# Unread matmuls in TensorE's pauses, the reciprocal roots spread from their column, and sums moved to VectorE, in a two-layer hybrid decoder trunk on one core

## The reference

```
for l in range(2):
    sh1, sc1, g1, sh2, sc2, g2 = split(silu(c) @ w_mod[l] + b_mod[l])
    p = (x * (1 + sc1) + sh1) @ w_in[l]                 # q k v qi ki wi xr yg
    attn = dsa_attention(rope(q), rope(k), v, ...)      # 4 heads, top 128 keys per query
    lru  = rg_lru(conv(xr)) * gelu(yg)                  # 512 wide
    merged = concat(rms_norm(attn, g_attn), rms_norm(lru, g_lru))
    x = layer_norm(alpha * x + (1 + g1) * (merged @ w_out[l]))
    h2 = x * (1 + sc2) + sh2
    x = layer_norm(alpha * x + (1 + g2) * (square(relu(h2 @ w_up[l])) @ w_down[l]))
```

## Time and profile before

| | |
|---|---|
| median of 3 runs | 1364.4 us (1359.66 to 1368.24) |
| the profiled execution | 1368.02 us, of which 1366.2 us are the span from its first to its last instruction |
| TensorE busy | 1300.0 us, 95% of the span |
| VectorE, ScalarE, GpSimd busy | 789.9, 552.0, 156.6 us |
| mean granted TensorE clock | 0.966 of full |
| HBM read | 155.64 MB, 115 GB/s over the span |

### The profile page before, as it was taken

How to read it: one execution, slowest core, us unless ns; L and a number is a source line. 1 busy time by engine, 2 the same in 40 slices (tenths; PEclk the granted TensorE clock), 3 DMA queues, 4 the chain that set the end, 5 groups by cost and what they waited for, 6 DMA issues and landing times.

```text
span 1366.2 us, 17071 instructions
## 1 busy us (share of the span) xinstructions
PE 1300.0 (95%) x6225; PEld 1025.0 (75%) x6225; DVE 789.9 (58%) x1298; ACT 552.0 (40%) x849; POOL 156.6 (11%) x129
## 2 busy tenths in 40 slices
PE   3999998899999999999999999988999999999996
PEld 2776766776888888888867776657868888888886
DVE  3656988556752734537466589874574344343353
ACT  3743455533632413324246335563273232231331
POOL 3000334001000000000120013510200000000012
PEclk9999998898999999999989999989999999999997
DMA  9743445211334243342244444520223323333311
GB/s 314 250 157 124 154 128 187 71 47 47 109 121 140 92 154 96 104 154 93 77 140 153 141 126 136 171 76 10 84 62 123 93 92 99 101 92 93 104 64 62
DMA packets 73397, 158.56 MB, mean 116 GB/s; under 512 B 6528, under 2 KB 10872, under 8 KB 73336
## 3 DMA queue, kind: packets, MB, share of 16 engines
q1 hardware_dynamic: 59904, 108.61, 25.5%
q0 software_dynamic: 12800, 48.76, 10.7%
q10 hardware_dynamic: 632, 0.39, 0.1%
HBM read 155.64 MB, written 2.10 MB: 115 GB/s over the span
## 4 chain that ended last, share of the span: by engine, by line
PE 90%; ACT 3%; DVE 3%; DMA 2%; issue 1%; POOL 0%; POOLq 0%; DVEq 0%; SPq 0%; ACTq 0%
PE bank L645 26%; PE bank L647 25%; PE bank L646 25%; PE bank L690 2%; DMA first_mod<-in_w_mod_dram 2%; PE bank L610 2%; PE bank L548 1%; PE bank L834 1%; PE bank L868 1%; PE bank L742 1%; PE bank L848 1%; DVE lru_gate L1694 1%; PE bank L878 1%; PE bank L905 1%; PE bank L568 1%
## 5 line engine op out<-in xcount | busy, mean ns | idle before, releaser
L1440 DVE TENSOR_TENSOR w_lo<-w_raw,w_hi 128x1024 fp32r<-128x1024 f32 (+1 forms) x192 | 207.7, 1098 | 340.5 <-ACT w_hi L984 340.5
L984 ACT ACTIVATE w_hi<-w_raw 128x1024 fp32r<-128x1024 f32 (+1 forms) x216 | 203.7, 960 | 469.7 <-PE bank L647 467.7
L645 PE MATMUL bank<-a_hi,w_hi 128*128 128x512 f32 x896 | 374.4, 418 | 9.6 <-DVE a_lo L1482 6.3
L646 PE MATMUL bank<-a_lo,w_hi 128*128 128x512 f32 x896 | 352.4, 393 | 0.0
L647 PE MATMUL bank<-a_hi,w_lo 128*128 128x512 f32 x896 | 352.2, 393 | 0.0
L645 PEld LDWEIGHTS bank<-a_hi,w_hi 128*128 128x128 f32 x896 | 170.0, 190 | 64.0 <-issue 26.7
L646 PEld LDWEIGHTS bank<-a_lo,w_hi 128*128 128x128 f32 x896 | 170.3, 190 | 40.9 <-issue 5.8
L645 PE MATMUL bank<-b_hi,w_hi 128*128 128x512 f32 x512 | 199.7, 390 | 0.0
L647 PE MATMUL bank<-b_hi,w_lo 128*128 128x512 f32 x512 | 199.3, 389 | 0.0
L646 PE MATMUL bank<-b_lo,w_hi 128*128 128x512 f32 x512 | 199.2, 389 | 0.0
L647 PEld LDWEIGHTS bank<-a_hi,w_lo 128*128 128x128 f32 x896 | 170.0, 190 | 36.9
(11 more groups left out here) (265 smaller groups left out, 1473.7 us busy)
## 6 DMA issues: line engine op xcount, KB each, us to landing
mod_raw<-in_w_mod_dram POOLq DMA_DIRECT2D x40, 1024.0 KB, 5.9
w_raw<-in_w_up_dram SPq DMA_DIRECT2D x64, 512.0 KB, 3.7
w_raw<-in_w_down_dram SPq DMA_DIRECT2D x64, 512.0 KB, 3.7
w_raw<-in_w_in_dram SPq DMA_DIRECT2D x48, 512.0 KB, 3.7
w_raw<-in_w_out_dram SPq DMA_DIRECT2D x16, 512.0 KB, 3.8
first_mod<-in_w_mod_dram SPq DMA_DIRECT2D x4, 1024.0 KB, 19.6
first_mod<-in_w_mod_dram POOLq DMA_DIRECT2D x4, 1024.0 KB, 15.2
x_in<-in_x_dram POOLq DMA_DIRECT2D x4, 512.0 KB, 14.4
```

The source lines that it names most:

```text
L645: mm(o, wh, hi(kk), start=first, stop=False)
L646: mm(o, wh, lo(kk), start=False, stop=False)
L984: last = af(hi, src, ACT.Copy)
L1440: last = tt(lo, src, hi.bitcast(F32), ALU.subtract)
```

## The change

Six edits, of which the first two are one idea.

1. `keep_busy(n, b)` issues n matmuls of 512 columns of an fp32r identity into a bank that nobody reads. `layer_norm` has 3 of them after the sums of `ln_q`, and 14 (`LN_FILL`) after the spread of the roots. Each of the units 0 to 7 of the attention has 2 ahead of `turned(u)`.
2. `spread` no longer multiplies `ones_d` by a diagonal. Four matmuls of 128 columns have one column of roots as their weights, read with a stride of 0, and the identity as the moving operand. `diag` and `diag_l` go; the semaphore `roots_ready` takes the place of `diag_done`.
3. VectorE adds the eighth tile too into `ln_s` (not for the last norm). TensorE has four one-column matmuls less in the sums and one 128x512 matmul less for the mean. The sums now come in the order `ln_q`, `ln_s`, last squares.
4. VectorE adds the four tiles of squares of the recurrent branch into one at units 12, 13 and 14; `lru_sums` has 4 matmuls instead of 16 and stands at unit 15.
5. The modulation pieces 14 and 15 stand after the attention units and after the spread for the recurrent branch instead of at units 6 and 9.
6. In `norms` the low part of tile 0 comes before `norm_tile(1)`.

```
+LN_FILL = 14
 def spread(b, name, l, src):
-    mm(banks[b][:, :], ones_d[:, :], src.rearrange("p t q -> p (t q)"), start=True, stop=True)\
-        .then_inc(full_s[b], 1)
+    for t in range(TT):
+        last = mm(banks[b][:, t * P:(t + 1) * P], src[:, t:t + 1].broadcast_to([P, P]), ident[:, :], start=True, stop=True)
+    last.then_inc(full_s[b], 1)
+
+def keep_busy(n, b=6):
+    for _ in range(n):
+        mm(banks[b][:, :], ident_r[:, :], ident_r[:, :].unsqueeze(1).broadcast_to([P, TT, P]), start=True, stop=True)
...
 def layer_norm(l, tail, n):
-    x_last = x[:, DK - 1, :]
+    pe.wait_ge(ln_q_s, n * (DK - 2) + 2)
+    pe.wait_ge(free_s[4], uses_before(4, "sums" + tail, l))
+    add(TT, ln_q, first=True)
+    pe.wait_ge(free_s[6], ...)          # bank 6 of the group before is read
+    keep_busy(3)
     pe.wait_ge(ln_s_s, n)
-    pe.wait_ge(free_s[4], uses_before(4, "sums" + tail, l))
-    add(0, ln_s, first=True)
-    pe.wait_ge(ln_q_s, n * (DK - 2) + 2)
-    add(TT, ln_q)
-    pe.wait_ge(free_s[7], ...)
-    add(0, x_last)
+    add(0, ln_s)
     pe.wait_ge(ln_sq_s, n * DK)
     add(TT, ln_sq[:, (DK - 1) % 2, :], stop=True).then_inc(full_s[4], 1)
     pe.wait_ge(free_s[5], uses_before(5, "mb" + tail, l))
-    mm(banks[5][:, :], ones_d[:, :], ln_s[:, :], start=True, stop=False)
-    mm(banks[5][:, :], ones_d[:, :], x_last, start=False, stop=True).then_inc(full_s[5], 1)
-    pe.wait_ge(diag_done, l * 3 + (3 if tail else 2))
-    spread(4, "rb" + tail, l, diag)
+    mm(banks[5][:, :], ones_d[:, :], ln_s[:, :], start=True, stop=True).then_inc(full_s[5], 1)
+    pe.wait_ge(roots_ready, l * 3 + (3 if tail else 2))
+    spread(4, "rb" + tail, l, stat[:, 3, :])
+    keep_busy(LN_FILL)
...
-    pe.wait_ge(sq_ready, l * LT + LT)
+    pe.wait_ge(sq_added, l * (LT - 1) + (LT - 1))
     for t in range(TT):
-        for m in range(LT):
-            last = mm(banks[4][:, t:t + 1], sq_l[:, m, ...], ones_d[:, 0:1], start=(m == 0), stop=(m == LT - 1))
+        last = mm(banks[4][:, t:t + 1], sq_l[:, 0, ...], ones_d[:, 0:1], start=True, stop=True)
...
-        if u in (3, 6, 9):
-            late_mod(l, 12 + u // 3)
-        if u == 14:
+        if u == 3:
+            late_mod(l, 13)
+        if u == 15:
             lru_sums()
+        if u < 8:
+            keep_busy(2, 4)
         turned(u)
...
+    late_mod(l, 14)
     turn_tile(0)()
     turn_tile(1)()
-    pe.wait_ge(diag_done, l * 3 + 1)
-    spread(4, "lrb", l, diag_l)
+    pe.wait_ge(roots_ready, l * 3 + 1)
+    spread(4, "lrb", l, mix_root[:, 0:TT])
+    late_mod(l, 15)
     group("out0", ...)
...
 # VectorE: ln_stats, the attention units, norms
-    step(v_.reciprocal(stat[:, 3, :], stat[:, 2, :]))
-    step.settle()
-    stt(diag[:, :, :], ident..., float(D), stat[:, 3, :]..., ALU.mult, ALU.mult).then_inc(diag_done, 1)
+    v_.reciprocal(stat[:, 3, :], stat[:, 2, :]).then_inc(roots_ready, 1)
...
+    if 12 <= u < 12 + LT - 1:
+        m = u - 11
+        ve.wait_ge(sq_ready, l * LT + (m + 1))
+        ...
+        tt(sq_l[:, 0, :], sq_l[:, 0, :], sq_l[:, m, :], ALU.add).then_inc(sq_added, 1)
...
     norm_tile(0)
     first_full(l, blk)
-    norm_tile(1)
     step.settle()
     a_lo_tile(l, blk, 0)
+    norm_tile(1)
```

More of the change, by code:

```diff
@@ L226, in trunk_kernel @@
         full = sb("unsplit", [P, 2, T], F32, full_at)
-        diag = sb("diag", [P, TT, P], F32, full_at)
-        diag_l = sb("diag_lru", [P, TT, P], F32, yg_at)
         mod_rows = sb("mod_rows", [P, T], F32, yg_at + K2)
@@ L294, in trunk_kernel @@
         attn_max, mask_ready = sem("attn_max"), sem("mask_ready")
-        attn_sq, root_diag_s = sem("attn_squared"), sem("root_diag_done")
+        attn_sq, root_diag_s = sem("attn_squared"), sem("root_roots_ready")
         lru_squared = sem("decay_squared")
         pv_done = sem("pv_done")
-        sq_ready = sem("squares_ready")
+        sq_ready, sq_added = sem("squares_ready"), sem("squares_added")
         ln_sq_s, ln_q_s, ln_s_s = sem("ln_squared"), sem("ln_q_added"), sem("ln_s_added")
         var_done, root_done = sem("var_done"), sem("root_done")
-        diag_done = sem("diag_done")
+        roots_ready = sem("roots_ready")
         loads_begun, turns_begun = sem("loads_begun"), sem("turns_begun")
@@ L744, in add @@
                     return last
-                x_last = x[:, DK - 1, :]
-                pe.wait_ge(ln_s_s, n)
-                pe.wait_ge(free_s[4], uses_before(4, "sums" + tail, l))
-                add(0, ln_s, first=True)
-                pe.wait_ge(ln_q_s, n * (DK - 2) + 2)
-                add(TT, ln_q)
[L752 to L755, removed]
-                add(0, x_last)
+                pe.wait_ge(ln_q_s, n * (DK - 2) + 2)
+                pe.wait_ge(free_s[4], uses_before(4, "sums" + tail, l))
+                add(TT, ln_q, first=True)
+                pe.wait_ge(free_s[6], uses_before(6, "down12", l, NC - 1) + 1 if tail else uses_before(6, "out12", l) + 1)
+                keep_busy(3)
+                pe.wait_ge(ln_s_s, n)
+                add(0, ln_s)
                 pe.wait_ge(ln_sq_s, n * DK)
@@ L872, in lru_sums @@
                 def lru_sums():
-                    pe.wait_ge(sq_ready, l * LT + LT)
+                    pe.wait_ge(sq_added, l * (LT - 1) + (LT - 1))
                     pe.wait_ge(free_s[4], uses_before(4, "lms", l))
                     for t in range(TT):
-                        for m in range(LT):
-                            last = mm(banks[4][:, t:t + 1], sq_l[:, m, t * P:(t + 1) * P], ones_d[:, 0:1],
-                                      start=(m == 0), stop=(m == LT - 1))
+                        last = mm(banks[4][:, t:t + 1], sq_l[:, 0, t * P:(t + 1) * P], ones_d[:, 0:1], start=True, stop=True)
                     last.then_inc(full_s[4], 1)
@@ L883, in layer @@
                 pe.wait_ge(rope_done, l * 13 + 13)
-                pe.wait_ge(free_s[4], uses_before(4, f"vt{HEADS - 1}", l) + 1)
+                pe.wait_ge(free_s[4], uses_before(4, "lms", l))
                 scores(0)
@@ L1531, in ln_sum @@
                     ins = tt(ln_s[:, :], ln_s[:, :], x[:, m, :], ALU.add)
-                    if m == DK - 2:
+                    if m == (DK - 2 if name == "down1" and l == DEPTH - 1 else DK - 1):
                         ins.then_inc(ln_s_s, 1)
@@ L1739, in layer @@
                         lru_scan(u - 7)
+                    if 12 <= u < 12 + LT - 1:
+                        m = u - 11
+                        ve.wait_ge(sq_ready, l * LT + (m + 1))
+                        if m > 1:
+                            ve.wait_ge(sq_added, l * (LT - 1) + (m - 1))
+                        tt(sq_l[:, 0, :], sq_l[:, 0, :], sq_l[:, m, :], ALU.add).then_inc(sq_added, 1)
                     if u in (6, 10, 14):
@@ L1795, in layer @@
                 token_diag(1)
-                stt(diag_l[:, :, :], ident[:, :].unsqueeze(1).broadcast_to([P, TT, P]), float(D),
-                   mix_root[:, 0:TT].unsqueeze(2).broadcast_to([P, TT, P]), ALU.mult, ALU.mult).then_inc(diag_done, 1)
+                ve.sem_inc(roots_ready, 1)
                 mix_vars(2)
@@ L1838, in run @@
                             residual(l, f"out{j}", m, 2)
-                            if m < DK - 1:
-                                ln_sum(l, f"out{j}", m)
+                            ln_sum(l, f"out{j}", m)
                     return run
@@ L1875, in run @@
                                 residual(l, f"down{j}", m, 5, c)
-                                if last and m < DK - 1:
+                                if last and (m < DK - 1 or l < DEPTH - 1):
                                     ln_sum(l, f"down{j}", m, c)
```

2 lines of the change are left out of this document (removed).

## The result

The changed kernel takes 1348.18 us (median of 4 runs, 1347.46 to 1349.79) against 1366.32 us (4 runs, 1359.66 to 1368.41): a ratio of 0.9876, 95% interval 0.9848 to 0.9904, so 18 us or 1.2% faster. The profiled execution took 1348.19 us with a span of 1346.3, 19.9 us less than the profiled execution of before, whose 1368.02 us were at the upper end of its runs. So a comparison of the two traces shows some 2 us more than the medians do.

The account below looks back on a forecast made before the run. The prediction took TensorE, 90% of the chain, as the bound, through its standstills and half-clock stretches. Norms 12.0, attention's end 9.1 and start 0 sum to 21.1 us; between 1346.9 and 1343.3 it took 1345 us, range 1338 to 1354.

Parts of the forecast that it names:

- Group starts after the norms: At the three norms, the next matmul group starts at E + 9.2, E ending the last group's matmuls; 6.7 us saved.
- Clock behind the norms: In the groups after the three norms, full clock instead of half gives back 6.4 us.
- the sum of 14.7: Whole-kernel saving instead of 21.1 us if recorded clock events were unreliable and the 6.4 us behind the norms dropped out.
- Can the group use it? ... yes, barely: Groups after norms: TensorE needs 2.7 us per tile, VectorE 2.06 plus two weight halves, so full clock is usable.
- The attention's end: Fewer one-column sums of squares and no half clock behind them save 5.2 us in layer 0, 3.9 in layer 1.
- The attention's start: First attention units: VectorE and table loads bind, so fills give 0; bounds 3.6 us cost to 0.6 saved a layer.
- my own signs of being wrong: Half clock during fills, a row maximum waiting for TensorE at units 3 to 7; table load due within 16 us.
- The late modulation: Two pieces of 1.05 us each, moved into TensorE's waits of 1.21 and 2.28 us near the attention's end.
- case B: Rival: the clock falls all the same, elsewhere or in two of three norms; 6.7 us lost, 1352; chance 0.20.
- A: Rival: the attention's fills lie on the path at full clock, up to 2 x 3.6 us, 1352; chance 0.15.
- D: Rival: unread matmuls don't hold the clock, fills run at half clock; net 15 us slower, 1379; chance 0.05.
- The rule on transposes: Transposes don't count as busy for the clock, leaving the values alone to hold it at the attention's end.

Follow-up runs that it names:

- e4: The changed kernel with ScalarE's first three weight splits for up1 ahead of its eight residual scalings: 1344.48 us, ratio 0.9854.
- e5: The kernel of e4 without the unread matmuls of the three norms: 1351.76 us, ratio 0.9898.
- e7: The changed kernel with the recurrent branch's squares summed by TensorE again, 16 one-column matmuls and no VectorE additions: 1358.76 us, ratio 0.9954.
- e10: The changed kernel with modulation pieces 14 and 15 back at units 6 and 9: 1352.89 us, ratio 0.991.
- e2: The changed kernel without the 16 unread matmuls of each attention, those of the norms kept: 1350.14 us, ratio 0.9884.
- the best kernel: The kernel of e4 with layer 1's residual scalings moved later and 11 unread matmuls after each norm's spread instead of 14: 1342.82 us.
- e6: The kernel before the change with the unread matmuls alone added, in norms and attention: 1361.16 us, ratio 0.9959.

## Why the prediction was right, and where its terms were off

The forecast was 21.1 us and 1345; measured were 18.1 and 1348.2, inside the range of 1338 to 1354. The profiled spans, which the 21.1 were worked out from, differ by 19.9. They give the terms one by one.

- **Group starts after the norms**: forecast 2.0 + 3.1 + 1.6 = 6.7; measured 2.1 + 2.1 + 1.7, 5.8 before rounding. The steps came as worked out: sums at E + 1.8 (1.5), reciprocal ending at E + 4.9 (4.8), spread in 1.16 us (1.03), start at E + 9.15 (9.2), and set by the fill. The norm between the layers is the exception, E + 10.25: its mean and spread fell into the window at half clock from 686.5. I had taken 1.1 us off for one such fall and it cost 1.1; but with the fills in place the clock fell inside 17 of the 27 norms traced, so that it was only one in this trace was not to be counted on.
- **Clock behind the norms**: forecast 3.0 + 1.7 + 1.7 = 6.4; measured 2.9 + 1.5 + 1.7 = 6.1 as shorter up0, qi and up0. So the recorded clock could be trusted here, and the sum of 14.7, which would hold if its records meant nothing, was the wrong one.
- **The step that failed** is "Can the group use it? ... yes, barely". I looked at VectorE's work for the same group and not at ScalarE's order behind it. The group did use it; the next one did not. up1 waited for its weights in both layers, 3.5 us, and xr of layer 1 lost 0.7. The norms therefore gave 7.7 and not 12.0 us. e4 shows the cause by turning the order round (-3.7), e5 that it hid the fills' worth (6 to 7.3 instead of 3.7). It was to be seen before the change: ScalarE's order is in the code, and 5.75 us of scalings ahead of a split that VectorE waited 5.91 us for stood in the trace of before as well.
- **The attention's end**: forecast 5.2 + 3.9 = 9.1; measured 5.4 + 4.3, 9.6 before rounding, from the table load at unit 6 to out0. e7 confirms that the sums of squares carry it, with the half clock behind them (8.5 us).
- **The attention's start**: forecast 0; measured +0.8 in layer 0 and -1.2 in layer 1, counted from the end of yg to the table load (238.46 against 237.73, with starts within 0.1 us). The sum is near zero, by luck: in layer 0 the clock fell at 232.35, in layer 1 it did not. Where it did not fall (e4, both layers) the load came 0.8 and 1.2 us sooner than before, more than the 0.6 that I had as the most. And in layer 0 my own signs of being wrong appeared: two fills at half clock, a row maximum at unit 6 that waited 0.43 us for TensorE (as it had before, for 0.59), and the table load 16.5 us after the first scores (221.97) instead of 16 at the most. What they cost is in these 0.8 us.
- **The late modulation**: I priced the move at nothing, as hidden in two waits. Hidden it was: from the table load to out0 e10 took 33.8 us in both layers, as e4 did. But it is worth 3 to 5 us as work that keeps the clock up ahead of out0 (e10). The 1.6 us by which out0 of layer 1 became shorter belong here; I had left them out of the sum and put them into case B with the opposite sign.
- **The rivals.** A (fills on the path at full clock) did not happen: its 0.8 us in layer 0 stand in a stretch at half clock and are gone in e4. B happened in one norm. D did not happen, but part of its mechanism did in another kernel: with mean, spread and some of the fill at half clock the group begins at E + 11.8 in e2, 2.7 us later than in the changed kernel. The rule on transposes, on which the Trainium skill ("TensorE: Matmul & The Clock Gate", Part 4: PE-mode transpose) would have made B likelier at the attention's end, was not put to the test: in the changed kernel the clock held there, with the modulation pieces in the pauses.

So the mechanism was right, with one step missing: the waits of 4.2 us that the change itself uncovered. That the total came as near as it did is in part luck, since 3.3 us that were not in the sum made up for them: out0 of layer 1 (1.6), the attention (1.0 more than forecast) and the end of the program (0.7, not explained).

## What to carry to other kernels

After a change that lets a group of matmuls start earlier and run faster, ask what the group behind it needs, and read the order of the engine that prepares it: work of 6 us that is not urgent, ahead of a step that is, takes the gain back, and an experiment on either edit alone then reads as if it were worth little. Short pauses ahead of dense work are better filled with work that has to be done anyway than with unread matmuls. In this kernel fills paid where dense matmuls followed (the norms); where another engine bound (the attention's first units) they gave nearly nothing within the stretch, though taking them out of the best kernel cost 5.4 us for a reason that is open. And where one trace of each kernel is kept, compare it stretch by stretch: much of a difference can lie in stretches that the edit didn't touch.

## What the runs showed of the hardware that was not expected

- Two pauses of 1.21 and 2.27 us with 3 us of small matmuls between them can go before a granted clock of 0.50 over the start of out0: so it was in both layers of e10 and in layer 1 of before, but not in layer 0 of before nor in e6, which have the same pauses. With 2.1 us of 8-row matmuls in them it stood at 1.00 in all 20 cases.
- Fills did not keep the clock from falling inside a norm (17 of 27), but it was back before the group behind began in all 27.
- The granted clock fell while TensorE's records show it busy throughout: for 3.4 us in both layers of e7, right behind 32 one-column instructions in 3.63 us.
- The time of one kernel falls into steps with where the clock falls: e2 ran at 1346.7 and 1347.4 with mean clocks of 0.983 and 0.982, and at 1352.9 and 1353.0 with 0.974. The kernel before has two levels too, 1360.0 to 1360.8 us with 0.972 and 1364 to 1371 with 0.964 to 0.970. The four runs of the changed kernel lie within 2.3 us.
- A matmul of 128 columns whose weights are one column read with stride 0 costs the same as with ordinary weights: 8 instructions in 1.06 us (L698) beside 16 in 2.05 (L907).
